# First stage of a decoder layer: w_ada by column pieces, three projection tiles at once, x transposed once

## The reference

```python
c_act = silu(c)
ada = c_act @ w_ada + b_ada                   # 6 parts of 1024: shift1, scale1, gate1, shift2, scale2, gate2
h = rms_norm(x, norm1_g) * (1.0 + scale1) + shift1
proj = h @ w_in                               # 2816 columns: q, k, v of attention; q, k, v, gate of retention
...                                           # q and k each divided by their head's rms, times a gain
x = x + gate1 * (concat(attention, retention) @ w_out)
h = rms_norm(x, norm2_g) * (1.0 + scale2) + shift2
x = x + gate2 * (square(relu(h @ w_mlp1)) @ w_mlp2)
```

## Time and profile before

| | |
|---|---|
| runs, us | 1233.11, 1232.85, 1233.01 |
| span of the profiled execution, its own time as far as the profile gives it | 1232.6 |
| PE busy | 1196.7 (97%) |
| DVE busy | 526.8 (43%) |
| ACT busy | 365.8 (30%) |
| POOL busy | 78.6 (6%) |
| DMA in the mean | 75 GB/s |

### The profile page before, as it was taken

How to read it: one execution, slowest core, us unless ns; L and a number is a source line. 1 busy time by engine, 2 the same in 40 slices (tenths; PEclk the granted TensorE clock), 3 DMA queues, 4 the chain that set the end, 5 groups by cost and what they waited for, 6 DMA issues and landing times.

```text
span 1232.6 us, 13979 instructions
## 1 busy us (share of the span) xinstructions
PE 1196.7 (97%) x5494; PEld 967.2 (78%) x5494; DVE 526.8 (43%) x740; ACT 365.8 (30%) x562; POOL 78.6 (6%) x99
## 2 busy tenths in 40 slices
PE   7499999999999999999999999999999999999998
PEld 7477777777777897678888888888888888888887
DVE  2868955554335866873322133322233221233211
ACT  7444333345434433432211022211122111122111
POOL 1221000000001112400000000000000000000000
PEclk9799999999999999999999999999999999999999
DMA  8647533333102202101111111211111211111222
GB/s 288 220 110 235 158 113 93 96 98 106 35 18 66 72 19 82 38 25 55 40 57 46 51 51 39 64 35 51 52 49 36 64 38 52 51 45 41 69 85 69
DMA packets 114236, 92.75 MB, mean 75 GB/s; under 512 B 11492, under 2 KB 104848, under 8 KB 113296
## 3 DMA queue, kind: packets, MB, share of 16 engines
q1 hardware_dynamic: 105984, 63.26, 16.9%
q0 software_dynamic: 8208, 28.88, 7.7%
HBM read 83.74 MB, written 8.39 MB: 75 GB/s over the span
## 4 chain that ended last, share of the span: by engine, by line
PE 84%; DVE 10%; ACT 3%; issue 2%; DMA 1%; POOL 0%; SPq 0%; DVEq 0%; ACTq 0%
PE ps L439 25%; PE ps L441 24%; PE ps L440 24%; DVE riq L1111 3%; PE ps L528 2%; PE ps L549 2%; DVE acc L1045 1%; PE ps L540 1%; DMA xin<-in_x_dram 1%; DVE ht L1305 1%; DVE x1t L1316 1%; DVE act_lo L1292 1%; DMA wada<-in_w_ada_dram 1%; PE ps L748 1%; PE ps L615 1%
## 5 line engine op out<-in xcount | busy, mean ns | idle before, releaser
L439 PE MATMUL ps<-act_hi,w_hi 128*128 128x512 f32 x928 | 369.1, 398 | 9.2 <-DVE act_lo L1092 5.9
L441 PE MATMUL ps<-act_hi,w_lo 128*128 128x512 f32 x928 | 362.4, 391 | 0.0
L440 PE MATMUL ps<-act_lo,w_hi 128*128 128x512 f32 x928 | 362.1, 390 | 0.0
L439 PEld LDWEIGHTS ps<-act_hi,w_hi 128*128 128x128 f32 x928 | 174.8, 188 | 52.9 <-issue 14.6
L441 PEld LDWEIGHTS ps<-act_hi,w_lo 128*128 128x128 f32 x928 | 174.6, 188 | 37.0
L440 PEld LDWEIGHTS ps<-act_lo,w_hi 128*128 128x128 f32 x928 | 174.8, 188 | 35.9 <-issue 1.2
L439 PE MATMUL ps<-hid_hi,w_hi 128*128 128x512 f32 x512 | 200.4, 391 | 0.8 <-DVE hid_lo L1336 0.8
L441 PE MATMUL ps<-hid_hi,w_lo 128*128 128x512 f32 x512 | 199.4, 389 | 0.0
L440 PE MATMUL ps<-hid_lo,w_hi 128*128 128x512 f32 x512 | 199.2, 389 | 0.0
L782 ACT ACTIVATE w_hi<-w_raw 128x1024 fp32r<-128x1024 f32 (+1 forms) x94 | 95.3, 1015 | 254.6 <-PE ps L441 247.5
L1334 DVE TENSOR_TENSOR rsq<-rel 128x1024 f32<-128x1024 f32 x32 | 39.2, 1225 | 186.6 <-ACT rel L974 186.5
(11 more groups left out here) (137 smaller groups left out, 984.6 us busy)
## 6 DMA issues: line engine op xcount, KB each, us to landing
w_raw<-in_w_mlp_dram SPq DMA_DIRECT2D x64, 512.0 KB, 3.9
wada<-in_w_ada_dram POOLq DMA_DIRECT2D x32, 512.0 KB, 4.6
w_raw<-in_w_in_dram SPq DMA_DIRECT2D x18, 512.0 KB, 3.9
wada<-in_w_ada_dram SPq DMA_DIRECT2D x7, 1024.0 KB, 9.4
xin<-in_x_dram SPq DMA_DIRECT2D x8, 512.0 KB, 5.2
x_spill<-xt POOLq DMA_DIRECT2D x8, 512.0 KB, 6.6
x1t<-x_spill POOLq DMA_DIRECT2D x8, 512.0 KB, 5.3
out_dram<-ost POOLq DMA_DIRECT2D x7, 512.0 KB, 4.1
```

The costliest lines, as they stand in the source:

```text
L439: pe.matmul(bank, wh, hi, start=first, stop=False)
L440: pe.matmul(bank, wh, lo, start=False, stop=False)
L441: return pe.matmul(bank, wl, hi, start=False, stop=last)
```

## The change

Everything lies in the first stage and in the tiles up to 18.

- Loads on SP: all of x first, and a block's slot is free once it has been transposed and squared. Then w_ada's first two parts in five chunks of columns (`ADA_CHUNKS`: 1, 1, 2, 2, 2 k-tiles of the output), for both parts at once. Chunks 3 and 4 wait until the chunk whose memory they take has been summed. Tiles 2 and 3 have raw, hi and lo buffers of their own.
- x is transposed once; VectorE copies it out. 1 / rms goes as a diagonal times a matrix of ones (`rms_spread`) to all partitions (`rbc`), half by half, and `hn = xt * rbc` is made on VectorE (first half and two k-tiles of the second) and on GpSimd (the rest).
- A chunk is summed over w_ada's rows on VectorE (`ada_rows_sum`, eight operations), summed over partitions by products with one column (`ada_columns`), and made into a1 and ada (`modulation`). ScalarE scales and shifts each k-tile twice, into act_hi and in place into hn. act_lo is VectorE's, and GpSimd's for k-tiles 3, 5 and 7.
- TensorE runs tiles 0, 1 and 2 together, k outermost, as the k-tiles come. The columns of the next chunk stand behind the first k-tile of each chunk.
- The norms start with tile 3 and run a tile later than before; those of tiles 4 and 5 both stand at tile 6. The other four parts of w_ada start at tile 7 with three steps per tile, and are turned at tiles 10, 13, 15 and 18.

The core of the diff, without the buffers' addresses, the semaphores, and the old code that the listing above shows:

```diff
+FIRST = 3
+ADA_CHUNKS = [(0, 1), (1, 1), (2, 2), (4, 2), (6, 2)]
+POOL_LO = (3, 5, 7)
...
+        ada_rows = [at(f"ada_rows{i}", [2, KT, nk * P], REG + off * KB)
+                    for i, ((k0, nk), off) in enumerate(zip(ADA_CHUNKS, (16, 24, 76, 16, 76)))]
+        acc1 = at("acc1", [2, KT, P], TMPB)
...
-        ADA_OPS = 2
-        ADA_TURN = {KT * (j + 1) // ADA_OPS + 1: j for j in range(4)}
-        assert max(ADA_TURN) < RV and NU == N_PROJ - T_ATT
+        ADA_OPS, ADA_T0 = 3, 7
+        ADA_TURN = {ADA_T0 + (KT * (j + 1) + ADA_OPS - 1) // ADA_OPS: j for j in range(4)}
...
+            for n in range(NB):
+                if n >= XS:
+                    sp.wait_ge(s_xtp, n - XS + 1)
+                    sp.wait_ge(s_ssq, n - XS + 1)
+                sp.dma_start(xin[:, n % XS, :], x[0, n * P:(n + 1) * P, :]).then_inc(s_xin[n], 16)
...
+                k0, nk = ADA_CHUNKS[i]
+                for j in range(2):
+                    sp.dma_start(ada_rows[i][:, j, b0:b1, :],
+                                 w_ada_k[:, b0:b1, j * D + k0 * P:j * D + (k0 + nk) * P]).then_inc(landed, 16)
...
+            load_rows(0, 0, KT, s_rows[0])
+            load(0, w_in_k[:, :, NQ * HEAD:NQ * HEAD + P])
+            load(1, w_in_k[:, :, NQ * HEAD + P:NQ * HEAD + 2 * P])
+            load_rows(1, 0, KT, s_rows[1])
+            load_q(2)
+            sp.wait_ge(s_ssq, NB)
+            load_rows(2, 0, HK, s_rows[2])
+            load_rows(2, HK, KT, s_rows2[2])
+            for i in (3, 4):
+                sp.wait_ge(s_acc, KT * (i - 1))
+                load_rows(i, 0, HK, s_rows[i])
+                load_rows(i, HK, KT, s_rows2[i])
+            sp.dma_start(cst[:, C_ONE:], consts[:, C_ONE:]).then_inc(s_cst, 16)
+            sp.wait_ge(s_acc, 4 * KT)
+            load_q(3)
...
-            for t in range(2):
-                pool.wait_ge(s_whi, t + 1)
-                pool.tensor_tensor(w_lo[:, t, :, :], w_raw[:, t, :, :], w_hi[:, t, :, :].bitcast(F32),
-                                   ALU.subtract).then_inc(s_wlo, 1)
-            for u in range(3, 2 * KT, 4):
...
+            pool.wait_ge(s_rbc, 2)
+            pool.wait_ge(s_xt, NB)
+            for k in range(2, KT):
+                pool.tensor_tensor(hn[:, k, HALVES[1]], xt[:, k, HALVES[1]], rbc[:, HALVES[1]], ALU.mult).then_inc(s_hnp, 1)
+            for k in POOL_LO:
+                pool.wait_ge(s_v1, k + 1)
+                pool.wait_ge(s_hi1, k + 1)
+                pool.tensor_tensor(act_lo[:, k, :], hn[:, k, :], act_hi[:, k, :].bitcast(F32),
                                    ALU.subtract).then_inc(s_act1p, 1)
...
-            pool.wait_ge(s_hnp, NB)
-            pool.wait_ge(s_ssq, NB)
-            pool.wait_ge(s_xt, NB)
+            pool.wait_ge(s_acc, ACC1)
...
+                pe.wait_ge(s_diag, half + 1)
+                if half == 0:
+                    pe.wait_ge(s_ct, 1)
+                pe.matmul(ps[:, 6 + half, :], one[:, :], flat(diag[:, half * HK:(half + 1) * HK, :]), start=True,
+                          stop=True).then_inc(s_rbp, 1)
...
+            for n in range(NB):
+                pe.wait_ge(s_xin[n], 16)
+                wait(pe, s_xt, n - 2)
+                for k in range(KT):
+                    tr = pe.transpose(ps[:, 2 * (n % 3) + k // 4, tokens(k % 4)], xin[:, n % XS, tokens(k)], ident)
+                tr.then_inc(s_xtp, 1)
+                if n == 5:
+                    rms_spread(0)
...
+                k0, nk = ADA_CHUNKS[i]
+                pe.wait_ge(s_acc, KT * (i + 1))
+                if i == 0:
+                    pe.wait_ge(s_rbc, 1)
+                for j in range(2):
+                    for k in range(nk):
+                        c = 4 * i + j * nk + k
+                        mm = pe.matmul(ps[:, 6, c:c + 1], acc1[:, j, k0 + k, :], one[:, 0:1], start=True, stop=True)
+                mm.then_inc(s_col, 1)
...
+            ada_columns(0)
+            for k in range(KT):
...
+                    pe.wait_ge(s_act1p, POOL_LO.index(k) + 1)
...
+                    pe.wait_ge(s_act1, k + 1 - sum(v < k for v in POOL_LO))
+                for t in range(FIRST):
+                    if k == 0:
+                        pe.wait_ge(s_wlo, t + 1)
+                        pe.wait_ge(s_vec if t == 2 else s_xt, 1 if t == 2 else NB)
+                    for half in range(2):
+                        mm = passes(ps[:, 2 * t + half, :], hi_of(t)[:, k, :], lo_of(t)[:, k, :], act_hi[:, k, HALVES[half]],
+                                    act_lo[:, k, HALVES[half]], k == 0, k == KT - 1)
...
+                for i, (k0, nk) in enumerate(ADA_CHUNKS):
+                    if i and k == ADA_CHUNKS[i - 1][0]:
+                        ada_columns(i)
...
+                        if (t, half, k) == (FIRST, 0, 4):
+                            pe.wait_ge(s_cst, 16)
+                            pe.wait_ge(s_evp, FIRST)
+                            qk_sums(TK)
+                        if (t, half, k) == (FIRST, 1, 4):
+                            qk_sums(TQ)
+                        if (half, k) == (0, 4) and FIRST < t <= T_ATT:
                             qk_sums(t - 1)
...
+                        mm = chain(ps[:, 6 + half, :], 0, act_hi, act_lo, HALVES[half], KT, 0, before, we_hi[1], we_lo[1])
...
+                wait_used(act, t - 4 if isinstance(t, int) and t in (4, 5) else t - 2, mlp)
...
+                act.wait_ge(s_ssq, (half + 1) * HK)
+                act.activation(sd8[:, half * HK:(half + 1) * HK], ss[:, half * HK:(half + 1) * HK], ACT.Sqrt, bias=eps[:, :],
+                               scale=1.0 / D).then_inc(s_sd, 1)
...
+                act.wait_ge(s_rbp, half + 1)
+                act.activation(rbc[:, HALVES[half]], ps[:, 6 + half, :], ACT.Copy).then_inc(s_rbc, 1)
...
+            for n in range(NB):
+                act.wait_ge(s_xin[n], 16)
+                wait(act, s_ssq, n)
+                act.activation(sqj[:, :], xin[:, n % XS, :], ACT.Square, accum_out=ss[:, n:n + 1]).then_inc(s_ssq, 1)
+                if n == HK - 1:
+                    rms_sd(0)
+                if n == NB - 2:
+                    rms_copy(0)
+            rms_sd(1)
...
+            split_next(1)
+            for k in range(KT):
+                i = max(v for v, (k0, nk) in enumerate(ADA_CHUNKS) if k0 <= k)
+                act.wait_ge(s_a1, 2 * (i + 1))
+                act.wait_ge(s_hn, KT + min(k, 1) + 1)
+                wait(act, s_hnp, k - 1)
+                act.activation(act_hi[:, k, :], hn[:, k, :], ACT.Identity, scale=a1[:, k:k + 1],
+                               bias=ada[:, k:k + 1]).then_inc(s_hi1, 1)
+                act.activation(hn[:, k, :], hn[:, k, :], ACT.Identity, scale=a1[:, k:k + 1],
+                               bias=ada[:, k:k + 1]).then_inc(s_v1, 1)
...
+            split_next(2)
+            for t in range(FIRST):
+                act.wait_ge(s_mmp, t + 1)
+                act.activation(proj[:, t, :], bank_pair(t), ACT.Copy).then_inc(s_evp, 1)
+                if t == TK:
+                    qk_squares(TK)
+            for t in range(FIRST, N_PROJ):
...
-                if 0 < t < T_ATT:
+                if t < T_ATT:
                     split_next(t)
-                if 0 < t <= T_ATT and t - 1 != TV:
+                if t == FIRST:
+                    qk_sd(TK)
+                    qk_squares(TQ)
+                elif t <= T_ATT:
+                    qk_sd(t - 2)
+                if t == T_ATT:
                     qk_sd(t - 1)
...
+                dve.wait_ge(s_xtp, n + 1)
+                dve.tensor_copy(xt[:, :, tokens(n)], bank_pair(n % 3).rearrange("p (k n) -> p k n", k=KT)).then_inc(s_xt, 1)
...
+                blocks = slice(half * HK, (half + 1) * HK)
+                link(dve.reciprocal(rs8[:, blocks], sd8[:, blocks]))
+                dve.tensor_tensor(diag[:, blocks, :], ident.unsqueeze(1).broadcast_to([P, HK, P]),
+                                  rs8[:, blocks].unsqueeze(2).broadcast_to([P, HK, P]), ALU.mult).then_inc(s_diag, 1)
...
+                dve.wait_ge(s_rbc, half + 1)
+                dve.wait_ge(s_xt, (half + 1) * HK)
+                dve.tensor_tensor(hn[:, k, HALVES[half]], xt[:, k, HALVES[half]], rbc[:, HALVES[half]],
+                                  ALU.mult).then_inc(s_hn, 1)
...
+                k0, nk = ADA_CHUNKS[i]
+                dst = acc1[:, :, k0:k0 + nk, :].rearrange("p j k n -> p j (k n)")
+                for b in range(KT):
...
+                        dve.wait_ge(s_acc, KT * i + b)
+                    row = ada_rows[i][:, :, b, :]
+                    if b == 0:
+                        dve.tensor_scalar(dst, row, ct[:, 0:1], None, ALU.mult).then_inc(s_acc, 1)
+                    else:
+                        dve.scalar_tensor_tensor(out=dst, in0=row, scalar=ct[:, b:b + 1], in1=dst,
+                                                 op0=ALU.mult, op1=ALU.add).then_inc(s_acc, 1)
...
+                dve.wait_ge(s_col, i + 1)
...
```

(57 more changed lines are left out.)

232 lines of the change are left out of this document (98 added, 134 removed).

## The result

The changed kernel takes 1261.37 us (median of four runs, 1260.52 to 1262.33) against 1232.94 (1232.85 to 1233.11): ratio 1.0232, 95% interval 1.0219 to 1.0244. It is 28.4 us slower. The forecast was 1254, with a range of 1240 to 1263.

A forecast was written before the change was run, and what follows sets the result against it. TensorE was taken as full from 53.7 us on, so only an earlier start or idle stretch moves the end. 8.8 + 9.2 + 1.8 + 1.0 + 0.5 = 21.3; 1232.6 + 21.3 + 0.4 = 1254 us, range 1240 to 1263.

The forecast's parts named there:

- x and its diagonal done at 20.8, first matmul at 42.9: Start of kernel: reciprocal and diagonal end at 20.8 us, VectorE's row then lets TensorE start at 42.9, 10.8 us earlier.
- The hold by GpSimd: Before the first matmul: GpSimd's six products run one at a time with VectorE's work, costing 7.7 us; bounds 0 and 7.7.
- the sum of chunk 0: Before the first matmul, on VectorE: eight dependent operations of 256 elements, 3.9 us.
- ScalarE's two passes: Before the first matmul: VectorE waits for ScalarE's two passes over 1,024 elements, 2.2 us.
- the 18% rival: GpSimd's operations find gaps and cost VectorE nothing, 12.3 us less: T 86.7, time 1242; chance 18%.
- Three tiles, k outermost: T at 99.0: First stage: T, the end of the first three projection tiles, comes at 99.0 us, 8.8 later than 90.2.
- The clock: First stage: nine matmuls at the half clock after each long wait, 1.8 us more; counted at the first start.
- From T to the scores 62.1: Tiles 3 to 6: scores wait for the norms, ending at T + 62.1; TensorE idles 6.4, tile 7 starts 9.2 later.
- the norm pair: Norms of tiles 4 and 5 both after tile 5: 16.2 us on VectorE, where one takes 8.1; TensorE idles 6.4.
- Turn 1.0, spill 0.5: Behind the scores: one late w_ada turn costs 1.04 us; the last x spill, in tile 9, costs 0.5, bounds 0 and 3.
- The 8% rival, clock down throughout: First stage: clock stays down, every k-tile takes 7.7 us, T moves by 17, time 1271; chance 8%.
- The faster rival: First stage: VectorE and ScalarE keep ahead of TensorE; T 70.0, time 1225; decides under 77.7 (90.2 - 12.5, later terms); chance 6%.

The follow-up runs named there:

- experiment 1: Changed kernel with GpSimd's six quotients replaced by six plain copies on ScalarE, output not the reference's: 1253.7 us, ratio 1.0178 to the kernel before.
- experiment 2: Changed kernel with GpSimd's six quotients done by VectorE itself ahead of the first sum: 1258.2 us, ratio 1.0207 to the kernel before.
- Experiment 4: Changed kernel with unused matmuls put into TensorE's waits to keep the clock up: 1256.43 us, ratio 1.0198 to the kernel before.
- Experiments 5: Changed kernel with tile 4's roots and norm moved one tile ahead, leaving only tile 5's norm before the scores: 1256.34 us, ratio 1.0187 to the kernel before.
- experiment 6: Kernel before with tile 4's roots and norm moved a tile back, so norms of tiles 4 and 5 both precede the scores: 1241.55 us, ratio 1.0085.
- experiment 7: Changed kernel rearranged: GpSimd out of the stage, two sums on TensorE, columns and norms earlier, two sums split: 1235.61 us, ratio 1.0018 to the kernel before.
- Experiment 8: Experiment 7's version with act_lo reordered, x spills issued together and sums split one operation earlier: 1224.87 us, ratio 0.9941 to the kernel before.

## Why the prediction was right, and where it was short

The direction and the mechanisms held; the time was 7.4 us short. It lies 1.6 us inside the upper bound of 1263, which the prediction does not work out from any row, and outside the forecast's own range of 1249 to 1260. That the range holds it is in part luck. Step by step:

- *x and its diagonal done at 20.8, first matmul at 42.9.* Measured 20.8 and 42.31. The 20.8 was partly luck: the last block of x went out at 11.6 and took 6.0 us to land where I had 3.5, but the block ahead of it had been turned in that time. The hold by GpSimd, 7.7 in the sum, came to 6.3 (10.84 + 1.35 less 5.50 + 0.35 in experiment 1), nearer to the upper bound that I took than to 0. It was too much by 1.4, which nearly made up for two terms that were too small: the sum of chunk 0 takes 4.5 without a hold where I had 3.9, and ScalarE's two passes 2.4 for 2.2. Experiments 1 and 2 settle the hold against the 18% rival. The Trainium skill (SBUF — State Buffer, "SBUF: two separate sides") has VectorE and GpSimd lock the shared ports for a whole instruction, where both of VectorE's inputs lie in SBUF; the row of 2.69 us at 66.28 agrees.
- *Three tiles, k outermost: T at 99.0.* Measured 104.0. From the first matmul to the start of k 5 it took 46.3 us where I had 43.7. Of these 2.6 us, 0.9 is two sets of TensorE's columns at the half clock (1.32 and 1.55 where I had 1.0 each), and about 1.4 is the sums: their operations follow each other in 0.59 and 0.86 us, not in 0.50 and 0.77, while the hold in two of them was 1.9 for 2.3. The k-tiles 5 to 7 then took 15.4 us for 12.4. The clock is the term that was mis-sized: I let it fall nine matmuls long at the first start alone. In fact 48 of the 144 tile matmuls of the stage were at the half clock, 9 and 8 behind the first two waits, 12 and 6 behind the next, 13 behind the last. Those beside VectorE's row cost little. The last 13, 0.2 us each, cost their full time, since no wait stood behind them. Experiment 4 gives the price: T 4.0 us earlier, 3.6 without that execution's earlier start. (The "55 us for 33 us of matmuls" of the prediction is a slip: 42.9 to 99.0 is 56.)
- *From T to the scores 62.1.* Measured 62.7, with TensorE's wait 6.07 for 6.4. Experiments 5 and 6 show that it is the norm pair. I had not counted the scores' own half clock (0.9). Behind them the clock took 1.9 (forecast 1.8).
- *Turn 1.0, spill 0.5.* Measured 1.1 and 0.5. The 0.5 was only what was left over after the slack: experiment 7 shows the same wait take 1.8 us where the rest is tighter.
- *The 8% rival, clock down throughout*, was half right: it went down behind every wait but came back each time. Where it put 17 us on T, experiment 4 measured about 4.
- *The faster rival* needed VectorE to keep ahead. It did not. Experiment 8 shows that this was a matter of what VectorE was given and in what order: with two sums moved to TensorE, GpSimd out and the other sums split around the act_lo, T fell to 79.4. That is still above the 77.7 under which that rival was to decide; the version is faster because the wait of the norm pair and the half clock behind it, 11.0 of the 12.5 us set against it, are gone too.

One execution's start is good to some 2 to 3 us only: experiment 6, with the code ahead of the matmuls unchanged, had its first at 51.18, against 53.74. The profiled execution of the kernel before was itself some 1.4 us longer than its median run (an estimate: in every run that has both, the time is 1.8 us above the span, so its span of 1232.6 stands for about 1234.4). Differences between two profiled executions, the 27.9 and 13.8 above included, carry that much.
